# Moved tile copies, four prologue means and an earlier split of the fourth gate weight in a two-layer decoder trunk

## The chip, the cores and the metric

The kernel runs on one core of one Trainium2 chip. The metric is the device time of one execution in microseconds, as a median of repeated runs. TensorE is the matrix engine, ScalarE, VectorE and GpSimd work on tiles of 128 partitions, SyncE (SP) issues the DMA transfers. Each engine goes through its own instructions in order, and they wait for each other by counting semaphores.

## The reference

```
for i in (0, 1):                       # 512 tokens, width 1024
    h = rmsnorm(x, norm_pre[i])
    y = fox_mixer(h) if i == 0 else conv_mixer(h)      # attention with forget gates; gated short convolution
    x = x + rmsnorm(y, norm_post[i])                   # residual update
    gate = sigmoid(rmsnorm(x, pe_norm[i]) @ pe_w_gate[i])
    x = x + gate * (p[i] @ pe_w_proj[i])               # p[i]: 256 wide, per-layer embedding
```

`fox_mixer` projects `h` to q, k, v, z and 16 forget gates, `conv_mixer` to four tensors of width 1024; both end with an output projection of 1024 x 1024. All is in float32.

## The kernel before, in words

The residual stream is kept transposed in `xT`, as KT = 8 tiles of 128 features by 512 tokens. Each float32 operand of a matrix product is split into a rounded high part (`_hi`) and a rest (`_lo`), and a product is three matmuls of 128x512: hi·hi, lo·hi, hi·lo (lines 1031 to 1033). A weight tile of 1024x128 (a *slot*) is loaded into one of two `w_raw` buffers, ScalarE casts it to one of four `w_hi` buffers (`weight_hi`, line 470), and GpSimd subtracts to get `w_lo` (`weight_lo`, line 410); in the output projection VectorE does this subtraction (`slot_lo`, line 894). A load waits until the slot two before it has its low part, and a cast waits until TensorE has done with the slot four before it.

**Prologue.** For each of the eight tiles ScalarE makes `act_hi` (line 489) and for six of them a square `x_sq` (line 492); VectorE makes `act_lo` (line 730), and squares tiles 3 and 5 itself (line 735) and adds tiles 2 and 4 to them (line 738). TensorE runs two matmuls per tile for the forget gates (lines 1055, 1056) and six mean matmuls with `mean_f`, a matrix of 1/1024, that sum the squares over features (line 1066; each counts as two instructions in the trace). Then come the first two projection steps (lines 1073 to 1077). Ahead of all of it ScalarE casts the gates' weights `f_w` (line 484), and TensorE runs eleven matmuls on constants.

**Tail of a layer.** Each layer ends with the output projection (eight steps of 24 matmuls), the embedding's projection `ple_tile` (eight tiles of six matmuls; four stay in PSUM, the last four go through the two banks `ps_pj` and are copied to `pleT` by `ple_copy`, line 652), and the gate stage: gate tiles 0, 1 and 2 side by side, feature tile by feature tile of `act`, as `act` comes (`side_by_side`), then a mean (`norm_mean`), then tiles 3 to 7 one after the other. While TensorE is in the embedding's projection, the residual update runs: ScalarE turns the mean of the squares into a scale (lines 498, 500), VectorE computes `t_a` = `yT` times scale (line 926) and `xT` += `t_a` (line 917), ScalarE makes `act_hi` (line 657) and squares (lines 614, 618), VectorE makes `act_lo` (line 921), and GpSimd adds the squares up (`add_square`, line 445). TensorE needs `act_lo` k for the k-th part of the gate tiles, and the sum for the mean behind them.

The orders of ScalarE and VectorE are written out by hand. In the update of the kernel before, ScalarE copies embedding tile 0 ahead of the first `act_hi`, tile 1 behind `act_hi` 0, tiles 2 and 3 behind `act_hi` 1 (`PLE_COPY_AT`), and casts the fourth gate weight (slot `SLOT_GATE[l] + 3`) behind the fifth square; GpSimd makes its low part behind its fourth addition. In the last layer the last gate tile is done in two halves of 256 tokens (`parts`): `gate_scale` (line 952) for both, and then, half by half, tanh on ScalarE (line 700), two VectorE instructions (lines 967, 970) and a store.

Of the kernel before, what the change touches and what calls it, by code (L numbers as in the profile page):

```python
# [82 lines left out]
GROUPS = 16  # L83
PLE_COPY_AT = {0: [1], 1: [2, 3]}
P_AT = 4
NORM_AFTER = KT - 3
PAIRED = {2: 3, 4: 5}
MEANS = [k for k in range(KT) if k not in PAIRED]
TURN_0_WEIGHTS = {5: [0], 8: [1], 14: [2, 3]}
# [20 lines left out]
def tile_step(first, m):  # L110

    return first + m - (m > WIDE)


def trunk(nc, xT_in, pT_in, weights, f_in, b_f_in, pre_in, post_in, pe_in, taps_in, outT):
# [6 lines left out]
    with ctx:  # L122
# [3 lines left out]
        def sem(name):  # L126
            return ctx.enter_context(nc.semaphore(name))
# [107 lines left out]
        x_sq_act = sem("x_sq_act")  # L235
        x_sq_dve = sem("x_sq_dve")
        x_pair = sem("x_pair")
        act_hi_done = sem("act_hi_done")
# [150 lines left out]
        def _(pool):  # L389
# [12 lines left out]
            def weight_lo(slot, place):  # L402

                pool.wait_ge(w_hi_done, slot + stream(place) - place + 1)
                if place in [slot + 3 for slot in SLOT_GATE]:

                    pool.wait_ge(w_ready, stream(place))
                for k in range(0, KT, LO_TILES):
                    tiles = slice(k, k + LO_TILES)
                    last = nc.gpsimd.tensor_tensor(w_lo[place % RING][:, tiles], w_raw[stream(place) % RAW][:, tiles],  # L410
                                                   w_hi[place % RING][:, tiles], ALU.subtract)
                last.then_inc(w_ready, 1)
# [34 lines left out]
            for l in range(2):  # L447
                for m in range(KT):
                    add_square(3 * KT * l + KT + m)
                    if m == 4:  # L450
                        weight_lo(SLOT_GATE[l] + 3, SLOT_GATE[l] + 3)
                for m in range(KT):
                    for slot in ([4, 5] if m == 0 else [m + 5]):
                        if slot < KT + 3 * (l == 0):
                            weight_lo(SLOT_GATE[l] + slot, SLOT_GATE[l] + slot)
                if l == 0:
                    with pool.Fori(0, KT) as m:
                        for j in range(4):
                            weight_lo(4 * m + SLOT_CONV + 3 + j, SLOT_CONV + 3 + j)
# [3 lines left out]
        def _(act):  # L463
# [18 lines left out]
            log_exp_tables()  # L482
            act.wait_ge(f_loaded, 16)
            nc.scalar.copy(f_w[:, :, 0:F_PART], f_raw[:]).then_inc(f_hi_done, 1)
            act.wait_ge(g_loaded[0], 16)
            for k in range(KT):

                act.wait_ge(x_loaded[k], 16)
                nc.scalar.activation(act_hi[0][:, k, :], xT[:, k, :], ACT.Copy, scale=g_pre[:, 0, k:k + 1]
                                     ).then_inc(act_hi_done, 1)  # L490
                if k not in PAIRED.values():
                    nc.scalar.activation(x_sq[k][:], xT[:, k, :], ACT.Square).then_inc(x_sq_act, 1)
            weight_hi(0, 0)
# [126 lines left out]
            for l in range(2):  # L620
# [4 lines left out]
                for m in range(KT):  # L625
# [17 lines left out]
                    if m == P_AT:  # L643
                        act.wait_ge(p_loaded, 16 * l + 16)
                        nc.scalar.copy(p_hi[:], p_in[:]).then_inc(p_hi_done, 1)
                norm_scale(3 * l + 1, ps_o[:])
                act.wait_ge(g_loaded[3], 16)
# [5 lines left out]

                ple_copy(0)
                for m in range(KT):
                    act.wait_ge(x_new, 2 * KT * l + m + 1)
                    nc.scalar.activation(a_g[:, m, :], xT[:, m, :], ACT.Copy, scale=g_pe[:, l, m:m + 1]  # L657
                                         ).then_inc(act_hi_done, 1)
                    for tile in PLE_COPY_AT.get(m, []):
                        ple_copy(tile)  # L660
                    square(3 * KT * l + KT + m, xT[:, m, :])
                    if m == 4:
                        weight_hi(SLOT_GATE[l] + 3, SLOT_GATE[l] + 3)

# [60 lines left out]
        @block.vector  # L725
        def _(dve):
            for k in range(KT):

# [3 lines left out]
                                               ).then_inc(act_ready, 1)  # L732
                if k in PAIRED.values():
                    pair = list(PAIRED.values()).index(k)
                    nc.vector.tensor_tensor(x_sq[k][:], xT[:, k, :], xT[:, k, :], ALU.mult).then_inc(x_sq_dve, 1)
                    dve.wait_ge(x_sq_act, k - pair)
                    dve.wait_ge(x_sq_dve, pair + 1)
                    nc.vector.tensor_tensor(x_sq[k][:], x_sq[k - 1][:], x_sq[k][:], ALU.add).then_inc(x_pair, 1)

# [146 lines left out]
            for l in range(2):  # L886
# [15 lines left out]
                for m in range(KT):  # L902
# [6 lines left out]
                    if m == P_AT:  # L909
                        dve.wait_ge(p_hi_done, l + 1)  # L910
                        nc.vector.tensor_tensor(p_lo[:], p_in[:], p_hi[:], ALU.subtract).then_inc(p_ready, 1)
                dve.wait_ge(rs_ready, 3 * l + 2)
                links = {}
# [24 lines left out]

                def gate_scale(m):
                    if m < WIDE:  # L940
# [7 lines left out]
                    else:  # L948
                        for i, tokens in enumerate(parts(l, m)):
                            s = tile_step(STEP_GATE[l], m) + i  # L950
                            dve.wait_ge(pj_done, s + 1)
                            nc.vector.tensor_tensor(t_a[m % 2][:, tokens], ps_pj[s % 2][:, tokens], rs[:, tokens],
                                                    ALU.mult).then_inc(pj_free[s % 2], 1)

                gate_scale(0)
                for m in range(KT):
                    if m == 0:
                        gate_scale(1)
                    elif m > 1:
                        gate_scale(m)  # L960
# [3 lines left out]
                    gated = t_a[m % 2] if m < PLE_STEPS else ps_ple[m - PLE_STEPS]  # L964
                    for i, tokens in enumerate(parts(l, m)):
                        dve.wait_ge(g_tanh, KT * l + m + i + 1)
                        link = chain(nc.vector.scalar_tensor_tensor(gated[:, tokens], t_b[m % 2][:, tokens], 1.0,
# [56 lines left out]
        def _(pe):  # L1024
# [28 lines left out]
            for k in range(KT):  # L1053
# [4 lines left out]
                if k == KT - 1:  # L1058
                    end.then_inc(f_done, 1)
                summed = sum(paired < k for paired in PAIRED.values())  # L1060
                if k in PAIRED.values():
                    pe.wait_ge(x_pair, summed + 1)
                elif k not in PAIRED:
                    pe.wait_ge(x_sq_act, k - summed + 1)
                if k in MEANS:
                    end = nc.tensor.matmul(ps_o[:], mean_f[:], x_sq[k][:], start=k == MEANS[0], stop=k == KT - 1)
            end.then_inc(ms_done, 1)
# [219 lines left out]
```

## Time and profile before

| | us |
|---|---|
| median of 3 runs | 648.5 (648.17 to 648.59) |
| the profiled execution | 647.84 |
| its span in the trace | 646.0 |
| TensorE busy | 632.9 (98%) |
| VectorE busy | 388.1 (60%) |
| ScalarE busy | 322.5 (50%) |
| GpSimd busy | 308.2 (48%) |

The span runs from the first instruction to the last, the execution's own time has a further 1.8 us around it. A line such as L921 is the line of the kernel. A row of a timeline gives the start and the duration, the engine, the line and the operation, what is written from what, and in brackets the idle time of the engine before it and who ended it. The chain is followed back from the last instruction, at each step to what released it.

### The profile page before, as it was taken

How to read it: one execution, taken by the hardware profiler on the slowest of the kernel's cores; microseconds unless marked ns; L12 is line 12 of the kernel's file. 1: busy time of each engine (PE TensorE's matmuls, PEld its weight loads, DVE VectorE, ACT ScalarE, POOL GpSimd, SP SyncE). 2: the span in 40 equal slices, each digit the busy share in tenths (PEclk: the TensorE clock that was granted, in tenths of full speed). 3: DMA queues.
4: the chain of work that ended last, by engine and by line, in shares of the span. 5: the costliest groups of instructions: out<-in, count | busy, mean ns of one | idle time of the engine just before them, and what ended most of it. 6: DMA issues, size and time to landing. Idle time of an engine off the chain costs nothing.

```text
span 646.0 us, 9283 instructions
## 1 busy us (share of the span) xinstructions
PE 632.9 (98%) x2932; PEld 517.4 (80%) x2932; DVE 388.1 (60%) x774; ACT 322.5 (50%) x557; POOL 308.2 (48%) x412
## 2 busy tenths in 40 slices
PE   8999999999999999999989999999999999999897
PEld 5788888888888888788767788888888887887686
DVE  5558678787878787455868635333434242456864
ACT  6748566565657575555665632321222122555451
POOL 1776554645545566000566558556544651001770
PEclk9999999999999999999999999999999999999999
DMA  6363334343334333153013223323222422350131
GB/s 203 109 203 109 107 106 134 116 110 111 116 112 127 125 106 107 33 195 131 2 60 104 97 74 122 117 78 130 74 94 92 129 99 97 97 164 32 33 131 65
DMA packets 27161, 68.69 MB, mean 106 GB/s; under 512 B 3568, under 2 KB 10096, under 8 KB 27136
## 3 DMA queue, kind: packets, MB, share of 16 engines
q1 hardware_dynamic: 27136, 68.37, 32.3%
q8 instruction: 14, 0.23, 0.2%
q14 instruction: 11, 0.09, 0.0%
HBM read 66.23 MB, written 2.13 MB: 106 GB/s over the span
## 4 chain that ended last, share of the span: by engine, by line
PE 90%; DVE 7%; ACT 2%; issue 1%; DMA 0%; SPq 0%; DVEq 0%
PE ps_pj L1031 25%; PE ps_pj L1033 25%; PE ps_pj L1032 25%; PE ps_tr L1040 3%; DVE act_lo L921 2%; PE ps_o L1142 2%; PE ps_o L1141 2%; PE ps_sc L1111 1%; DVE xT L917 1%; PE ps_sc L1109 1%; PE ps_tr L1031 1%; PE ps_tr L1033 1%; PE ps_tr L1032 1%; DVE t_a L926 1%; PE ps_o L1046 1%
## 5 line engine op out<-in xcount | busy, mean ns | idle before, releaser
L410 POOL TENSOR_TENSOR w_lo<-w_raw,w_hi 128x256 fp32r<-128x256 f32 x324 | 253.5, 816 | 127.4 <-ACT w_hi L470 117.9
L1031 PE MATMUL ps_pj<-act_hi,w_hi 128*128 128x512 f32 (+1 forms) x728 | 290.2, 399 | 5.4 <-DVE act_lo L921 4.3
L1033 PE MATMUL ps_pj<-act_hi,w_lo 128*128 128x512 f32 (+1 forms) x728 | 282.8, 389 | 0.0
L1032 PE MATMUL ps_pj<-act_lo,w_hi 128*128 128x512 f32 (+1 forms) x728 | 282.7, 388 | 0.0
L1031 PEld LDWEIGHTS ps_pj<-act_hi,w_hi 128*128 128x128 f32 x728 | 137.0, 188 | 36.5 <-DVE act_lo L921 7.9
L1033 PEld LDWEIGHTS ps_pj<-act_hi,w_lo 128*128 128x128 f32 x728 | 136.8, 188 | 28.7
L1032 PEld LDWEIGHTS ps_pj<-act_lo,w_hi 128*128 128x128 f32 x728 | 137.2, 188 | 24.5 <-issue 0.7
L470 ACT CAST w_hi<-w_raw 128x1024 fp32r<-128x1024 f32 x96 | 100.5, 1048 | 92.5 <-DMA w_raw<-in_weights 69.7
L445 POOL TENSOR_TENSOR acc<-acc,sq 128x512 f32<-128x512 f32 x14 | 21.3, 1525 | 115.4 <-ACT sq L618 114.6
L418 POOL TENSOR_TENSOR bias<-bias,future 128x128 f32<-128x128 f32 x64 | 32.1, 533 | 76.0 <-DMA bias<-negc_scratch 76.0
L525 ACT ACTIVATE logit<-logit,nmax 128x128 f32<-128x128 f32 (+1 forms) x64 | 36.0, 563 | 46.4 <-DVE nmax L766 46.0
L781 DVE TENSOR_TENSOR pt_lo<-ps_tr,pt_hi 128x128 fp32r<-128x128 f32 (+1 forms) x64 | 30.8, 483 | 9.7 <-ACT pt_hi L535 8.9
L894 DVE TENSOR_TENSOR w_lo<-w_raw,w_hi 128x1024 fp32r<-128x1024 f32 x15 | 18.4, 1226 | 25.2 <-ACT w_hi L470 25.2
L766 DVE CUSTOM_DVE_ANT_0 logit<-ps_sc,bias 128x128 f32<-128x128 f32 (+1 forms) x64 | 31.2, 488 | 3.0 <-issue 1.5
L775 DVE TENSOR_SCALAR logit<-logit,rrec 128x128 f32<-128x128 f32 (+1 forms) x64 | 30.3, 473 | 2.3
L535 ACT CAST pt_hi<-ps_tr 128x128 fp32r<-128x128 f32 (+1 forms) x64 | 26.8, 423 | 4.7 <-PE ps_tr L1040 3.8
L1040 PE MATMUL ps_tr<-ident,logit 128*128 128x128 f32 x160 | 28.2, 275 | 0.1
L1008 DVE TENSOR_TENSOR cv_z<-ps_pj,rs 128x512 f32<-128x512 f32 x8 | 5.5, 692 | 38.0 <-PE ps_pj L1033 38.0
L827 DVE TENSOR_TENSOR q_lo<-scaled,q_hi 64x512 fp32r<-64x512 f32 x32 | 26.5, 828 | 1.9 <-ACT q_hi L565 1.5
L1040 PEld LDWEIGHTS ps_tr<-ident,logit 128*128 128x128 f32 x160 | 20.6, 140 | 7.7 <-DVE logit L775 1.4
L988 DVE TENSOR_TENSOR cv_w<-ps_pj,cv_c 128x512 f32<-128x512 f32 x8 | 5.5, 692 | 31.2 <-PE ps_pj L1033 31.1
L921 DVE SCALAR_TENSOR_TENSOR act_lo<-xT,g_pe,act_hi 128x512 fp32r<-128x512 f32 x16 | 20.9, 1317 | 5.2 <-ACT act_hi L657 5.2
(143 smaller groups left out, 741.4 us busy)
## 6 DMA issues: line engine op xcount, KB each, us to landing
w_raw<-in_weights SPq DMA_DIRECT2D x100, 512.0 KB, 3.4
bias<-negc_scratch SPq DMA_DIRECT2D x16, 256.0 KB, 7.4
bias<-negc_scratch SPq DMA_DIRECT2D x16, 192.0 KB, 6.2
xT<-in_xT SPq DMA_DIRECT2D x8, 256.0 KB, 4.4
bias<-negc_scratch SPq DMA_DIRECT2D x16, 128.0 KB, 4.8
out<-xT SPq DMA_DIRECT2D x7, 256.0 KB, 2.0
bias<-negc_scratch SPq DMA_DIRECT2D x16, 64.0 KB, 3.4
p_in<-in_pT SPq DMA_DIRECT2D x2, 512.0 KB, 4.6
```

The source lines that it names most:

```text
L410: last = nc.gpsimd.tensor_tensor(w_lo[place % RING][:, tiles], w_raw[stream(place) % RAW][:, tiles], w_hi[place % RING][:, tiles], ALU.sub ...
L418: nc.gpsimd.tensor_tensor(diagonal, diagonal, future[:], ALU.add).then_inc(bias_ready[h], 1)
L470: nc.scalar.copy(w_hi[place % RING][:], w_raw[position % RAW][:]).then_inc(w_hi_done, 1)
L525: nc.scalar.activation(logit[b][:, 0:n], logit[b][:, 0:n], ACT.Exp, scale=-1.0, bias=nmax[:, b:b + 1], accum_out=rsum[:, b:b + 1]).then_in ...
L766: nc.vector.tensor_tensor_reduce(out=logit[b][:, 0:n], in0=ps_sc[u % 2][:, 0:n], in1=bias[h][:, i, 0:n], scale=-1.0, scalar=3e38, op0=ALU. ...
L775: nc.vector.tensor_scalar(logit[b][:, 0:n], logit[b][:, 0:n], rrec[:, b:b + 1], None, ALU.mult).then_inc(prob_ready, 1)
L781: nc.vector.tensor_tensor(causal(pt_lo, i), ps_tr[n % TR_BANKS][:, 0:(i + 1) * P].rearrange("p (k c) -> p k c", c=P), causal(pt_hi, i), AL ...
L921: nc.vector.scalar_tensor_tensor(a_g[1][:, m - 1, :], xT[:, m - 1, :], g_pe[:, l, m - 1:m], a_g[0][:, m - 1, :], ALU.mult, ALU.subtract).t ...
L1031: nc.tensor.matmul(out, w_h, a[0][:, k, tokens], start=k == first, stop=False)
L1032: nc.tensor.matmul(out, w_h, a[1][:, k, tokens], start=False, stop=False)
L1033: end = nc.tensor.matmul(out, w_l, a[0][:, k, tokens], start=False, stop=k == last)
L1040: last = nc.tensor.transpose(ps_tr[n % TR_BANKS][:, t * P:(t + 1) * P], tile, ident[:])
```

## The change

- ScalarE's prologue: `act_hi` 0 goes first, the cast of `f_w` behind it; ScalarE squares all eight tiles.
- VectorE no longer squares; it adds up squares 0 and 1, then 2 and 1's sum into 3, then 4 into 5 (four additions). TensorE runs four means, for tiles 3, 5, 6 and 7.
- Residual update, in both layers: the copies of the embedding tiles 0, 1 and 3 stand behind `act_hi` 1, 2 and 3, the one of tile 2 behind square 2.
- The fourth gate weight is cast by ScalarE ahead of the norm's scale, and VectorE makes its low part ahead of the update, where GpSimd did so in the midst of it.
- The last gate tile of the last layer: each half is scaled right ahead of its own gating, instead of both halves first.

```diff
-PLE_COPY_AT = {0: [1], 1: [2, 3]}
+PLE_COPY_AT = {1: [0], 2: [1], 3: [3]}
+PLE_COPY_BEHIND = {2: [2]}
-PAIRED = {2: 3, 4: 5}
-MEANS = [k for k in range(KT) if k not in PAIRED]
+SUMS = {1: [0], 3: [2, 1], 5: [4]}
+MEANS = {3: 3, 5: 4}
...
             def weight_lo(slot, place):
 
                 pool.wait_ge(w_hi_done, slot + stream(place) - place + 1)
-                if place in [slot + 3 for slot in SLOT_GATE]:
+                if place in [slot + 4 for slot in SLOT_GATE]:
 
                     pool.wait_ge(w_ready, stream(place))
...
                     add_square(3 * KT * l + KT + m)
-                    if m == 4:
-                        weight_lo(SLOT_GATE[l] + 3, SLOT_GATE[l] + 3)
...
             log_exp_tables()
-            act.wait_ge(f_loaded, 16)
-            nc.scalar.copy(f_w[:, :, 0:F_PART], f_raw[:]).then_inc(f_hi_done, 1)
             act.wait_ge(g_loaded[0], 16)
             for k in range(KT):
 
                 act.wait_ge(x_loaded[k], 16)
                 nc.scalar.activation(act_hi[0][:, k, :], xT[:, k, :], ACT.Copy, scale=g_pre[:, 0, k:k + 1]
                                      ).then_inc(act_hi_done, 1)
-                if k not in PAIRED.values():
-                    nc.scalar.activation(x_sq[k][:], xT[:, k, :], ACT.Square).then_inc(x_sq_act, 1)
+                if k == 0:
+                    act.wait_ge(f_loaded, 16)
+                    nc.scalar.copy(f_w[:, :, 0:F_PART], f_raw[:]).then_inc(f_hi_done, 1)
+                nc.scalar.activation(x_sq[k][:], xT[:, k, :], ACT.Square).then_inc(x_sq_act, 1)
...
+                weight_hi(SLOT_GATE[l] + 3, SLOT_GATE[l] + 3)
                 norm_scale(3 * l + 1, ps_o[:])
...
-                ple_copy(0)
                 for m in range(KT):
...
                     square(3 * KT * l + KT + m, xT[:, m, :])
-                    if m == 4:
-                        weight_hi(SLOT_GATE[l] + 3, SLOT_GATE[l] + 3)
+                    for tile in PLE_COPY_BEHIND.get(m, []):
+                        ple_copy(tile)
...
-                if k in PAIRED.values():
-                    pair = list(PAIRED.values()).index(k)
-                    nc.vector.tensor_tensor(x_sq[k][:], xT[:, k, :], xT[:, k, :], ALU.mult).then_inc(x_sq_dve, 1)
-                    dve.wait_ge(x_sq_act, k - pair)
-                    dve.wait_ge(x_sq_dve, pair + 1)
-                    nc.vector.tensor_tensor(x_sq[k][:], x_sq[k - 1][:], x_sq[k][:], ALU.add).then_inc(x_pair, 1)
+                for other in SUMS.get(k, []):
+                    dve.wait_ge(x_sq_act, k + 1)
+                    wait(dve, x_sum, added)
+                    nc.vector.tensor_tensor(x_sq[k][:], x_sq[other][:], x_sq[k][:], ALU.add).then_inc(x_sum, 1)
+                    added += 1
...
+                slot_lo(SLOT_GATE[l] + 3)
                 dve.wait_ge(rs_ready, 3 * l + 2)
...
                 for m in range(KT):
+                    whole = len(parts(l, m)) == 1
                     if m == 0:
                         gate_scale(1)
-                    elif m > 1:
+                    elif m > 1 and whole:
                         gate_scale(m)
...
                     for i, tokens in enumerate(parts(l, m)):
+                        if not whole:
+                            gate_scale(m, i)
                         dve.wait_ge(g_tanh, KT * l + m + i + 1)
...
                 if k in MEANS:
-                    end = nc.tensor.matmul(ps_o[:], mean_f[:], x_sq[k][:], start=k == MEANS[0], stop=k == KT - 1)
+                    pe.wait_ge(x_sum, MEANS[k])
+                elif k >= 6:
+                    pe.wait_ge(x_sq_act, k + 1)
+                if k in MEANS or k >= 6:
+                    end = nc.tensor.matmul(ps_o[:], mean_f[:], x_sq[k][:], start=k == 3, stop=k == KT - 1)
```

## Rows read from the trace of the kernel before

**Rows 1.** The chain that ended last: its share of the span by engine.
```profile
PE 90%; DVE 7%; ACT 2%; issue 1%; DMA 0%; SPq 0%; DVEq 0%
```

**Rows 2.** The chain in order of time, prologue: start, us, what.
```profile
1.19 0.42 SPq L334
...
1.66 2.93 DMA f_raw<-in_f_weights
...
5.64 0.52 ACT x_sq L492
6.16 0.61 ACT act_hi L489
...
11.23 1.32 DVE act_lo L730 x2
...
14.01 1.13 PE ps_o L1066 x2
...
16.91 0.86 PE ps_o L1066 x2
...
21.41 1.81 PE ps_pj L1077 x8
```

**Rows 3.** The same chain, around the gate stages: start, us, what.
```profile
312.71 0.59 ACT pleT L652
...
328.44 0.50 PE ps_pj L1031
...
332.81 0.86 PE ps_o L1046 x2
...
613.40 0.86 PE ps_o L1046 x2
```

**Rows 4.** Timeline of all engines, the last half tile.
```profile
641.87 0.42 DVE L952 TENSOR_TENSOR t_a<-ps_pj,rs 128x256 f32<-128x256 f32 x1 [2.45 <-PE ps_pj L1033]
...
642.33 0.42 ACT L700 ACTIVATE t_b<-t_a 128x256 f32<-128x256 f32 x1 [2.46 <-DVE t_a L952]
...
643.46 0.42 DVE L970 SCALAR_TENSOR_TENSOR xT<-ps_tr,xT 128x256 f32<-128x256 f32 x1
```

**Rows 5.** Timeline of ScalarE, layer 0, norm and start of the update.
```profile
303.83 0.60 ACT L498 ACTIVATE ln_ms<-ps_o 128x512 f32<-128x512 f32 x1 [1.73 <-PE ps_o L1046]
...
308.69 0.59 ACT L652 COPY pleT<-ps_pj 128x512 f32<-128x512 f32 x1 [3.62 <-PE ps_pj L1033]
309.17 0.73 ACT L657 ACTIVATE act_hi<-xT,g_pe 128x512 fp32r<-128x512 f32 x1
```

**Rows 6.** Timeline of VectorE, layer 0, residual update.
```profile
305.10 0.69 DVE L926 TENSOR_TENSOR t_a<-yT,ps_o 128x512 f32<-128x512 f32 x1 [2.85 <-ACT ps_o L500]
...
316.39 1.07 DVE L917 TENSOR_TENSOR xT<-xT,t_a 128x512 f32<-128x512 f32 x1
317.39 1.78 DVE L921 SCALAR_TENSOR_TENSOR act_lo<-xT,g_pe,act_hi 128x512 fp32r<-128x512 f32 x1
```

**Rows 7.** Timeline of GpSimd, layer 0, residual update.
```profile
313.90 4.71 POOL L445 TENSOR_TENSOR acc<-acc,sq 128x512 f32<-128x512 f32 x3 [55.06 <-ACT sq L618]
...
320.27 4.17 POOL L410 TENSOR_TENSOR w_lo<-w_raw,w_hi 128x256 fp32r<-128x256 f32 x4
```

**Rows 8.** Groups of instructions by line (x count, busy us, mean ns).
```profile
L470 ACT CAST w_hi<-w_raw 128x1024 fp32r<-128x1024 f32 x96 | 100.5, 1048 | 92.5 <-DMA w_raw<-in_weights 69.7
...
L894 DVE TENSOR_TENSOR w_lo<-w_raw,w_hi 128x1024 fp32r<-128x1024 f32 x15 | 18.4, 1226 | 25.2 <-ACT w_hi L470 25.2
```

**Rows 9.** Timeline of the DMA queue of SP, layer 0.
```profile
297.16 0.33 SPq L321 DMA_DIRECT2D w_raw<-in_weights  x1
```

**Rows 10.** The loads of line 321, 280 to 400 us: issue to landing.
```profile
DMA to landing us min/median/max: 3.2/3.3/5.6
```

**Rows 11.** DMA issue of the norm gains: x count, KB, us to landing.
```profile
g_pre<-in_norm_pre SPq DMA_DIRECT2D x1, 8.0 KB, 2.5
```

**Rows 12.** Stages: us, busy us of PE, PEld, DVE, ACT, POOL; clock, DMA.
```profile
13.00:14.00 1.00, 0.33 (x2) 0.00 (x0) 0.90 (x3) 0.99 (x2) 0.00 (x0) 1.00 0.00 0
```

More of the change, by code:

```diff
@@ L235, in trunk @@
         x_sq_act = sem("x_sq_act")
-        x_sq_dve = sem("x_sq_dve")
-        x_pair = sem("x_pair")
+        x_sum = sem("x_sum")
         act_hi_done = sem("act_hi_done")
@@ L726, in _ @@
         def _(dve):
+            added = 0
             for k in range(KT):
@@ L937, in gate_rest, with gate_scale @@
                         add_square(2 * KT + m)
-                def gate_scale(m):
+                def gate_scale(m, i=0):
                     if m < WIDE:
@@ L948, in gate_scale @@
                     else:
[L949 to L953, printed above, removed]
+                        s = tile_step(STEP_GATE[l], m) + i
+                        tokens = parts(l, m)[i]
+                        dve.wait_ge(pj_done, s + 1)
+                        nc.vector.tensor_tensor(t_a[m % 2][:, tokens], ps_pj[s % 2][:, tokens], rs[:, tokens],
+                                                ALU.mult).then_inc(pj_free[s % 2], 1)
                 gate_scale(0)
                 for m in range(KT):
+                    whole = len(parts(l, m)) == 1
                     if m == 0:
                         gate_scale(1)
-                    elif m > 1:
+                    elif m > 1 and whole:
                         gate_scale(m)
@@ L1059, in _ @@
                     end.then_inc(f_done, 1)
[L1060 to L1064, printed above, removed]
-                if k in MEANS:
-                    end = nc.tensor.matmul(ps_o[:], mean_f[:], x_sq[k][:], start=k == MEANS[0], stop=k == KT - 1)
+                if k in MEANS:
+                    pe.wait_ge(x_sum, MEANS[k])
[3 more added lines that the diff above has]
+                    end = nc.tensor.matmul(ps_o[:], mean_f[:], x_sq[k][:], start=k == 3, stop=k == KT - 1)
             end.then_inc(ms_done, 1)
```

## Prediction

> **What bounds the kernel now.** I read the chain that ended last first. It lies on TensorE for nine tenths [rows 1], so a change pays only where the chain leaves TensorE. Read in order of time, it does that in three kinds of place that this change touches. In the prologue it runs through ScalarE and VectorE to the sixth `act_lo`, and reaches the first projection's matmul at 17.77 [rows 2]. Between a layer's output projection and its gate stage it runs through VectorE's residual update, until the seventh `act_lo` releases TensorE at 328.44; the mean behind the gate's first three tiles starts at 332.81 in layer 0 and at 613.40 in layer 1 [rows 3]. At the end it is the last half tile's gating [rows 4]. The timelines of ScalarE, VectorE and GpSimd in the second place then show why VectorE is late there [rows 5 to 7].
>
> **Residual update, twice: what goes.** Today ScalarE takes `ple_copy(0)` ahead of the first `act_hi`. That copy waits 3.62 us for TensorE, runs at 308.69, and `act_hi` follows at 309.17 [rows 5], though the first new `xT` was there at about 306.5 (the first `t_a` starts at 305.10 and takes 0.69 with the update as long behind it [rows 6]). After the change ScalarE can write `act_hi` 0 at 306.5 to 307.1, some 2.7 us earlier. The second thing that goes is the fourth gate weight's low part on GpSimd, 4.17 us in the middle of the update [rows 7].
>
> What GpSimd costs VectorE must be worked out, because GpSimd's seven additions per layer stay. An `xT` update takes 0.69 us alone and 1.07 beside GpSimd; an `act_lo` took 1.78 there [rows 6], where its chain piece in the prologue, without GpSimd, is 1.32/2 = 0.66 [rows 2]. `t_a`, whose second input is in PSUM, is not stretched. Three additions in a row take 4.71 us [rows 7] with two VectorE instructions of about 0.6 let in between, so one holds the path for (4.71 - 1.2)/3 = 1.17, call it 1.2 us. The two engines take turns, whole instructions at a time. The Trainium skill says the same and more strongly (SBUF — State Buffer, "SBUF: two separate sides"): the pair of ports is an exclusive lock, held for the whole instruction, also against a VectorE instruction with two SBUF inputs. By that rule every addition that meets such an instruction delays it until it ends; by a mere stretching in proportion, an addition would cost some 0.5 us and the update would end about 2 us earlier than below. The walk below takes turns as the rows do.
>
> **The walk through layer 0.** VectorE per tile is `xT` 0.61, `act_lo` 0.66, `t_a` 0.61 and gaps, 2.0 us. From 305.10 [rows 6]: `xT` 0 and 1 done at 306.45 and 307.75, `act_lo` 0 at 308.4, 1 at 310.35. The first square is at ScalarE's end at 309.7, behind the moved copy 0; its addition gets its turn at 310.35 to 311.55. Taking turns from there (additions 2 to 6 at 312.15, 314.0, 317.75, 319.6 and 322.7, each 1.2; an `xT` or `act_lo` that is ready meanwhile waits, a square is ready about 1.3 behind its `xT`), `act_lo` 2 ends at 314.0, 3 at 316.5, 4 at 319.6, 5 at 322.1, 6 at 325.2 and 7 at 325.85, and the last addition at 327.0. TensorE: 8 x 9 = 72 matmuls for three tiles side by side, at 1.81/8 = 0.226 us [rows 2]. The first three run at once, the fourth needs the bank of copy 3, which starts at 312.71 and takes 0.59 [rows 3]. That copy now stands behind `act_hi` 3, whose `xT` comes at 312.15, so it still runs at about 312.75; the fourth matmul ends at some 313.9, a restart included, and without a stall the other 68 end at 329.3. Tile 6 is then wanted at 329.3 - 18 x 0.226 = 325.2, just as it comes; with 0.2 for a restart the mean starts at 329.5 in place of 332.81, **3.3 us earlier**. Bounds: no stall gives 3.5. If each of the six additions ahead of `act_lo` 6 cost its whole 1.2 us (308.4 + 6 x 2.0 + 7.2 = 327.6 in place of 328.44), 0.85 us is left. I take 3.3, since an addition that falls on `t_a` costs about half. The mean needs all additions (327.0), so it is not the next wait. Layer 1 has the same walk: 6.6 us for both.
>
> **What is added ahead of the update.** ScalarE gets one weight cast of 1.05 us and VectorE one low part of 1.23 [rows 8]. Before `ln_ms` at 303.83 ScalarE waits 1.73 us [rows 5], so the cast fits at 302.1 to 303.1 if its load has landed. The load is issued at 297.16 [rows 9] and loads take 3.2 to 5.6 us there, 3.3 in the median [rows 10], thus 300.5. VectorE does its part at 303.2 to 304.4, and sits idle for the 2.85 us before 305.10 [rows 6]. Cost nothing, with 0.7 us to spare on both; queued behind is the whole update, so past 302.8 a late load would cost one for one. Of the moved copies, 1 frees its bank at about 310.85, and TensorE starts the tile that needs it six matmuls before 312.71, at 311.3; 2 frees its own at 311.9 for the gate's first tile, which starts at about 312.5. Both are in time. SP issues no more than before: the load two slots on starts earlier, since the fourth weight's parts are ready 20 us sooner, and nothing waits for it.
>
> **Prologue.** ScalarE no longer waits for `f_raw` (4.59, from 1.66 + 2.93 [rows 2]) before `act_hi` 0. The norm gains land at 1.19 + 2.5 = 3.7 [rows 2, 11], tile 0 issued before them too. So `act_hi` 0 runs 3.75 to 4.4, the cast of `f_w` 4.6 to 4.9, square 0 to 5.45. Tile 1's `act_hi` stands at 6.16 in the chain now, straight behind a square; its load sets some start between 5.45 and that, I take 5.85. From there one tile is 0.61 + 0.52 = 1.13 us [rows 2], eight squares instead of six (+1.04 us of ScalarE): `act_hi` 7 ends at 13.25, square 7 at 13.8, the first weight at 14.8. VectorE loses two squares and two sums and gets four sums, 4 instructions for 4, each of 0.69 (the form of [rows 6]). Its order gives the third sum at 10.85, `act_lo` 4 and 5 at 11.5 and 12.2, sum 4 at 12.85, `act_lo` 6 and 7 at 13.5 and 14.15. TensorE has four means of 0.86 instead of six, 1.7 us less: mean 3 starts at 10.9 and takes 1.13 as one behind a wait does, two tiles of gates at 0.46 each, then mean 5 at 12.95, gate 6, mean 6, gate 7, mean 7 until 16.45, in place of 16.91 + 0.86 = 17.77 [rows 2]. **1.3 us earlier.** Bounds: 0.5 if every handover costs a further 0.1, 1.6 if all that is gone is the two means. `ms_done`, the forget gates' chain, GpSimd's low parts and the loads behind them are released by this and move with it; the first low part has 3.6 us of matmuls before its use, so it does not become the wait.
>
> **Tail.** Today the first half's two instructions stand between the last `t_a` half (641.87) and the second half's [rows 4]. After: 641.87 + 0.42, tanh to 642.75, two instructions of 0.42 with gaps, 643.66 in place of 643.88. 0.2 us (0 to 0.5).
>
> **Sum.** 1.3 + 6.6 + 0.2 = 8.1 us. The profiled execution took 647.84 with a span of 646.0; it becomes 639.7. The median of the runs is 0.66 above it, so I predict **640.4 us**.
>
> **Rivals.**
> 1. The additions pace the update: they now begin four microseconds sooner and may meet VectorE on every tile. Against it, only `xT` and `act_lo` are stretched in the rows. Gain 0.85 per layer, in all 1.3 + 1.7 + 0.2 = 3.2: 645.3. Chance 0.13.
> 2. TensorE's clock falls in the prologue. Its work between 7 and 11 us thins to eight short matmuls, with a wait of about 1 us ahead of mean 3. Against it: it was busy for 0.33 of a microsecond at 13 to 14 and the granted clock stayed 1.00, the 2.4 GHz level [rows 12]. At the 1.2 GHz level the 5.55 us of work from 10.9 on would cost 2.8 to 5.6 more: 643.2 to 646.0. The Trainium skill (TensorE: Matmul & The Clock Gate, "Why this matters for your kernels") warns that idle gaps between bursts send the clock back; the row so far speaks for a safe gap. Chance 0.08.
> 3. Part is given back later: a gate step or a weight load in layer 0 doesn't follow, a load of 5.6 us in place of 3.3 [rows 10] takes 2.3 us: 642.7. For each later wait I find a releaser that moves too, which speaks against it. Chance 0.10.
> 4. Slower: the fourth weight's load lands late and its cast holds `ln_ms`, at its new place ahead of the norm. It costs nothing until 302.8 and then one for one in both layers. To lose 8.1 us and 1.3 more it would have to land (8.1 + 1.3)/2 = 4.7 us after that, 10.3 us from its issue; the longest is 5.6 [rows 10]. Chance 0.04, about 650.5.
> 5. No change: VectorE's update isn't what the gate stage waits for, 648.5. The release at 328.44 speaks against it. Chance 0.03.
>
> **Numbers.** My forecast holds 0.62, by itself 638.9 to 642.2. The range of 638.8 to 644.5 takes in rivals 2 (its nearer half) and 3 and leaves out 1, 4 and 5. Within 0.2%, 1.3 us, is about what a measurement can't tell from no change. Faster: 0.62 + 0.13 + 0.08 + 0.10 = 0.93; same 0.03; slower 0.04.
>
> **What would show it.** Right: first projection matmul at about 16.5; `act_hi` 0 of the update some 2.7 us earlier against `ln_ms`; no wait for `act_lo` on TensorE above 0.4 us in the gate stages; from `ln_ms` (303.83) to the mean (332.81) 25.6 us in place of 29.0; the last half tile's store alone at the end. Wrong: `act_lo` still of 1.2 to 1.8 us with TensorE waiting behind it (rival 1), matmuls of twice the length about 11 us (2), `ln_ms` later than 1 us behind its mean (4), or a gate stage shortened and a longer wait behind it (3).

## The result and the profile after

The changed kernel took 641.75 us in the median of four runs (639.91 to 642.9), the kernel before 648.34 beside it: a ratio of 0.9895, with a 95% interval of 0.9872 to 0.9919. Forecast were 640.4 us and a range of 638.8 to 644.5. The median is thus 6.6 us lower, where 8.1 were forecast. The four runs had a mean granted clock of 0.997 (641.69 us), 0.997 (642.9), 1.0 (641.8) and 0.998 (639.91). The profiled execution took 641.69 us with a span of 639.9, 6.1 us shorter than before.

The chain that ended last, by engine and by line, says first where VectorE's share of 7% went:

```profile
PE 91%; POOL 3%; issue 2%; DVE 1%; ACT 1%; DMA 1%; SPq 0%; POOLq 0%; DVEq 0%
```

VectorE has left the chain but for 1%; GpSimd's 3% are new, and lie between 20 and 44 us. Now the same chain in order of time around the gate stages and at the end, as in [rows 3, 4]:

```profile
303.69 0.86 PE ps_o L1048 x2
...
330.23 0.86 PE ps_o L1048 x2
...
580.90 0.86 PE ps_o L1048 x2
...
607.46 0.86 PE ps_o L1048 x2
635.94 0.43 DVE t_a L951
636.40 0.43 ACT t_b L698
636.85 0.44 DVE ps_tr L969
637.32 0.42 DVE xT L972
```

From the update's mean to the gate's mean it is 26.54 and 26.56 us, where it was 332.81 - 302.94 = 29.87 and 613.40 - 583.51 = 29.89: 3.33 us less in each layer, 6.66 for both. In the last half tile (`ps_tr` and `xT` are its two VectorE instructions) the last update ends at 637.74, 1.80 behind its `t_a`; in [rows 4] it was 643.88 - 641.87 = 2.01, so 0.21 less. Between the first gate mean and the update's mean of layer 1 nothing has moved, 250.67 us against 250.70. That leaves the start, and there the kernel is later than before: the update's mean of layer 0 comes 0.75 us after 302.94. Here is the prologue in the stages' view (us, then busy us of PE, PEld, DVE, ACT, POOL, the granted clock and DMA) and in TensorE's timeline:

```profile
6.00:7.00 1.00, 0.68 (x2) 0.19 (x2) 0.40 (x1) 1.00 (x3) 0.00 (x0) 1.00 0.96 336
7.00:8.00 1.00, 0.59 (x2) 0.19 (x2) 1.00 (x3) 1.00 (x3) 0.00 (x0) 1.00 1.04 385
8.00:9.00 1.00, 0.42 (x3) 0.19 (x2) 0.75 (x2) 1.00 (x3) 0.00 (x0) 1.00 1.07 406
9.00:10.00 1.00, 0.68 (x4) 0.19 (x2) 1.00 (x2) 1.00 (x3) 0.00 (x0) 1.00 1.04 416
10.00:11.00 1.00, 0.35 (x2) 0.00 (x0) 0.90 (x3) 1.00 (x2) 0.00 (x0) 1.00 1.05 430
11.00:15.00 4.00, 3.93 (x7) 1.86 (x8) 3.27 (x6) 3.82 (x7) 0.04 (x1) 0.57 0.12 50
15.00:17.77 2.77, 2.77 (x11) 1.41 (x9) 0.00 (x0) 0.34 (x1) 2.76 (x4) 1.00 0.00 0
```

```profile
11.07 1.80 PE L1067 MATMUL ps_o<-x_sq,mean_f 128*128 128x512 f32 x2 [0.72 <-DVE x_sq L735]
11.88 1.42 PE L1057 MATMUL ps_sc<-act_hi,f_w 128*64 128x512 f32 x1
13.09 0.63 PE L1058 MATMUL ps_sc<-act_lo,f_w 128*64 128x512 f32 x1
13.52 0.63 PE L1057 MATMUL ps_sc<-act_hi,f_w 128*64 128x512 f32 x1
...
17.69 0.79 PE L1074 MATMUL ps_pj<-act_hi,w_hi 128*128 128x512 f32 x1
```

From 6 to 11 us TensorE is busy for a third to two thirds of each microsecond, and then the granted clock falls to its lower level: 0.57 in the mean of 11 to 15 us, 1.00 again from there. The mean behind the wait takes 1.80 us where [rows 2] has 1.13, a matmul of 512 columns 0.63 in the timeline (0.43 in the chain) where it had 0.39 (0.23). The durations of neighbours overlap in a timeline, and the chain counts each share once. The mean ahead of the first projection matmul ends at 17.77 in the chain of before, and at 18.26 here.

### The profile page after: what moved, and what is told of

Its sections match the earlier page's. It is cut to its first block, busy times and chain, and to the rows that moved or that the text cites. A ratio compares the mean times of both kernels' runs of the same rounds, so it can differ in the third digit from the quotient of the medians.

```text
span 639.9 us, 9274 instructions
## 1 busy us (share of the span) xinstructions
PE 629.9 (98%) x2928; PEld 516.4 (81%) x2928; DVE 385.4 (60%) x776; ACT 324.1 (51%) x559; POOL 298.8 (47%) x404
## 4 chain that ended last, share of the span: by engine, by line
PE 91%; POOL 3%; issue 2%; DVE 1%; ACT 1%; DMA 1%; SPq 0%; POOLq 0%; DVEq 0%
PE ps_pj L1033 25%; PE ps_pj L1035 25%; PE ps_pj L1034 25%; PE ps_tr L1042 3%; POOL w_lo L410 2%; PE ps_o L1143 2%; PE ps_o L1142 2%; PE ps_sc L1112 1%; PE ps_tr L1033 1%; PE ps_tr L1035 1%; PE ps_tr L1034 1%; PE ps_sc L1110 1%; PE ps_o L1067 1%; PE ps_o L1048 1%; DMA xT<-in_xT 1%
## 5 line engine op out<-in xcount | busy, mean ns | idle before, releaser
L410 POOL TENSOR_TENSOR w_lo<-w_raw,w_hi 128x256 fp32r<-128x256 f32 x316 | 241.1, 796 | 132.7 <-ACT w_hi L468 132.7
L418 POOL TENSOR_TENSOR bias<-bias,future 128x128 f32<-128x128 f32 x64 | 33.9, 561 | 73.2 <-DMA bias<-negc_scratch 73.2
L892 DVE TENSOR_TENSOR w_lo<-w_raw,w_hi 128x1024 fp32r<-128x1024 f32 x17 | 20.8, 1226 | 26.2 <-ACT w_hi L468 26.2
L825 DVE TENSOR_TENSOR q_lo<-scaled,q_hi 64x512 fp32r<-64x512 f32 x32 | 24.1, 754 | 1.9 <-ACT q_hi L563 1.5
L785 DVE TENSOR_TENSOR o_u<-ps_o,o_half 64x512 f32<-64x512 f32 x16 | 11.0, 688 | 22.7 <-ACT o_half L542 22.5
```

The source lines that it names most:

```text
L418: nc.gpsimd.tensor_tensor(diagonal, diagonal, future[:], ALU.add).then_inc(bias_ready[h], 1)
```

## The experiments

The first four kernels below (`filled` to `prologue_only`) ran on one chip and the other eight on another. The kernel before took 648.01 us on the first, 647.93 and 647.86 on the second, and 648.34 beside the result; each median stands beside before's on the same chip.

**Where the clock comes in: four changes of the prologue.** `filled` gives TensorE something to do while it waits:

```diff
                 if k == KT - 1:
                     end.then_inc(f_done, 1)
+                for _ in range({0: 3, 1: 2, 2: 1, 3: 3}.get(k, 0)):
+                    nc.tensor.matmul(ps_tr[1][:, 0:P], mean_f[:], mean_f[:], start=True, stop=True)
```

> The changed kernel with nine more matmuls of 128x128 in the prologue, behind the forget gates' matmuls of tiles 0 to 3, three, two, one and three of them; their results are used nowhere. Theory (the clock fell because TensorE had too little to do between 6 and 11 us): the granted clock stays at 1.00 over 11 to 15 us, the first mean takes 0.86 to 1.13 instead of 1.80, the first projection matmul starts at about 16.5 instead of 18.26, and the median is 1.6 to 1.9 us below the changed kernel's, about 640.0, with less spread from run to run. Rival (the clock falls for another cause, or the delay is ScalarE's): no change, or 0.2 to 1 us slower for the extra work: 641.8 to 642.8.

Measured: 640.74 us (639.2 to 641.82, four runs), before 648.01; ratio 0.9882 (0.9867 to 0.9896). The mean granted clock was 0.999 or 1.0 in each run, and the first projection matmul was at 16.70 in the timeline, where the changed kernel had 17.69. So the clock held in these four runs, and in the prologue of the profiled one the microsecond came back. In time this does not show: 7.3 us below before is between the changed kernel's 6.6 and the 8.1 of its second measurement (`after_again` below), and the intervals overlap. The spread did not shrink, though that was expected too. The profiled execution, at 641.82 the slowest, shows another loss, behind the prologue (who TensorE waited for, 17 to 68 us; and its timeline there):

```profile
PE ps_tr L1042 <- DVE logit L773: 1.2, 1, 1.2
```

```profile
51.29 0.66 PE L1042 MATMUL ps_tr<-ident,logit 128*128 128x128 f32 x4 [1.18 <-DVE logit L773]
```

`logit` is a tile of attention weights, which VectorE normalises (line 773) ahead of TensorE's transposes. The same view of the kernel before shows no wait for it. It is taken up below.

`six_means` keeps TensorE busy with work that is wanted anyway, and spares VectorE two sums:

```diff
-SUMS = {1: [0], 3: [2, 1], 5: [4]}
-MEANS = {3: 3, 5: 4}
+SUMS = {3: [2], 5: [4]}
+MEANS = {3: 1, 5: 2}
...
-                elif k >= 6:
+                elif k not in (2, 4):
                     pe.wait_ge(x_sq_act, k + 1)
-                if k in MEANS or k >= 6:
-                    end = nc.tensor.matmul(ps_o[:], mean_f[:], x_sq[k][:], start=k == 3, stop=k == KT - 1)
+                if k not in (2, 4):
+                    end = nc.tensor.matmul(ps_o[:], mean_f[:], x_sq[k][:], start=k == 0, stop=k == KT - 1)
```

> The changed kernel with six means again (tiles 0, 1, 3, 5, 6, 7) and two sums on VectorE, all eight squares on ScalarE. Clock theory: the two means lie at 7 to 9 us and keep TensorE busy, so the clock stays at 1.00; mean 3 waits for one sum instead of three and starts at about 10.2, and the first projection matmul comes at 16.2 to 16.6: median 639.7 to 640.3. Rival (what costs is ScalarE's longer order): as the changed kernel, 641.7.

Measured: 639.89 us (638.68 to 640.48), before 648.01; ratio 0.9872 (0.9857 to 0.9886), no clock below 0.999. The median lies 8.1 us below before with two means more of work; against the changed kernel's 0.9895 (0.9872 to 0.9919) the intervals overlap, and the two are set side by side further down.

`old_prologue` is the changed kernel with the prologue of before, `prologue_only` the reverse; both diffs are those of the change, taken apart.

> The changed kernel with the prologue of the kernel before. Clock theory: the clock does not fall, the first projection matmul is at 17.77 as before, both gate stages gain 3.3 and the tail 0.2: 648.34 - 6.8 = 641.5, that is 0.2 us below the changed kernel and less spread. Rival (the prologue gained its 1.3 us and something later lost it): 643.0.

Measured: 641.14 us (640.93 to 641.43), before 648.01; ratio 0.9897 (0.9883 to 0.9911). The rest of the change gives 6.87 us, and all runs lie within 0.5 us.

> The kernel before with only the prologue of the change. Clock theory: the first projection matmul at 18.2 instead of 17.77 and a further 0.4 by the transfers that move with it: 648.5 to 649.3, with a spread of some 2 us between runs as the changed kernel has. Rival (the prologue gained 1.3 us): 647.0.

Measured: 647.58 us in the median of twelve runs, before 648.01; ratio 1.0003 (0.9991 to 1.0015), no difference (in the mean 648.02, before 647.89). But they fall in two groups: eight with a mean clock of 0.999 or 1.0 at 646.48 to 648.56, 647.2 in the mean, and four with 0.994 to 0.997 at 649.01 to 650.36, 649.6 in the mean. The theory's two halves are both there, a gain of 0.7 us against before's mean, and 2.4 us more in the runs that lost the clock, and I had mistaken how they mix: I expected every run late. The profiled one kept its clock; its first projection matmul is at 16.45 in the timeline, against 17.21 before.

**Which edit shortens the gate stages.** `copies_only` is the kernel before with `PLE_COPY_AT`, `PLE_COPY_BEHIND` and their loops changed as in the change; `weight_only` with the casts and low parts of the fourth gate weight moved alone.

> The kernel before with only the embedding copies moved. Theory (turns on one path between VectorE and GpSimd): act_hi 0 comes 2.7 us sooner, the fourth weight's 4.17 us on GpSimd still stand in the middle and delay tiles 5 and 6; act_lo 6 comes some 2 to 2.7 us earlier: 4.0 to 5.4 us for both layers, 642.6 to 644.0 where before stands at 648.0. Rival (the copies alone suffice, TensorE is the bound at once): 3.3 a layer, 641.4.

Measured: 644.45 us (644.03 to 644.72), before 647.93; ratio 0.9946 (0.9933 to 0.996): 3.5 us, less than theory (4.0 to 5.4) and rival (6.6) had. From the update's mean to the gate's, the chain has 331.43 - 303.26 = 28.17 us, 1.7 less than before.

> The kernel before with only the fourth gate weight's cast and low part moved. Theory: the start of the update stays, GpSimd loses 4.17 us of its 15.3 in it; the tile period falls from 2.9 to 2.7 for two tiles and the pile of additions goes: 0.4 to 1.0 us a layer, 646.0 to 647.2. Rival (GpSimd's low part was the main cost): 2.5 to 3.3 a layer, 641.4 to 643.0. A rival on the other side: the cast ahead of the norm's scale holds it, 648.5 or more.

Measured: 645.16 us (644.12 to 645.59), before 647.93; ratio 0.9958 (0.9945 to 0.9972): 2.8 us, twice the middle of the 0.8 to 2.0 that I gave it, and less than the rival's 5.0 to 6.6; from mean to mean it is in layer 0 331.60 - 302.95 = 28.65, 1.2 less, in layer 1 28.39, 1.5 less. VectorE's timeline shows by what. First `copies_only`, then `weight_only`, both in layer 0:

```profile
316.12 0.74 DVE L923 SCALAR_TENSOR_TENSOR act_lo<-xT,g_pe,act_hi 128x512 fp32r<-128x512 f32 x1
...
318.11 1.79 DVE L923 SCALAR_TENSOR_TENSOR act_lo<-xT,g_pe,act_hi 128x512 fp32r<-128x512 f32 x1
...
320.52 1.22 DVE L919 TENSOR_TENSOR xT<-xT,t_a 128x512 f32<-128x512 f32 x1
321.66 1.23 DVE L923 SCALAR_TENSOR_TENSOR act_lo<-xT,g_pe,act_hi 128x512 fp32r<-128x512 f32 x1
...
323.52 1.77 DVE L919 TENSOR_TENSOR xT<-xT,t_a 128x512 f32<-128x512 f32 x1
325.21 3.46 DVE L923 SCALAR_TENSOR_TENSOR act_lo<-xT,g_pe,act_hi 128x512 fp32r<-128x512 f32 x2
```

```profile
317.62 1.78 DVE L919 SCALAR_TENSOR_TENSOR act_lo<-xT,g_pe,act_hi 128x512 fp32r<-128x512 f32 x1
...
321.03 0.74 DVE L919 SCALAR_TENSOR_TENSOR act_lo<-xT,g_pe,act_hi 128x512 fp32r<-128x512 f32 x1
...
323.01 1.78 DVE L919 SCALAR_TENSOR_TENSOR act_lo<-xT,g_pe,act_hi 128x512 fp32r<-128x512 f32 x1
...
326.41 1.62 DVE L919 SCALAR_TENSOR_TENSOR act_lo<-xT,g_pe,act_hi 128x512 fp32r<-128x512 f32 x2
```

With the low part still on GpSimd (its four pieces run from 319.29 to 323.49, two additions back to back right behind them until 326.42), each `act_lo` and each `xT` update from 320.5 us on is held: 1.22 and 1.23 beside the pieces, 1.77 and 3.46 for two beside the additions. Only `t_a` keeps its 0.67. Without it `act_lo` 3 and 5 are held (1.78), while 4 takes 0.74 and the last two 1.62 together. The two edits add up to 6.3 us of the 6.9; neither makes TensorE the bound by itself.

> The kernel before with only the last gate tile's halves reordered. Theory: 0.2 us, 647.8 where before stands at 648.0, not to be told from no change by time; in the trace 0.22 us less between the last matmul and the last update. Rival (nothing, since the store ends last): 0.0.

Its edit is that of `gate_scale` and its calls. Measured: 647.67 us in the median of eleven runs (647.16 to 648.15), before 647.93; ratio 0.9997 (0.9988 to 1.0006). By time it is no difference; in its own chain the last update ends 643.72 - 641.93 = 1.79 us behind the start of the last `t_a`, 0.22 less than the 2.01 of [rows 4].

**Is it the thin work that makes the clock fall?** `two_means_out` takes two means away from the kernel before and touches nothing else:

```diff
-                if k in MEANS:
-                    end = nc.tensor.matmul(ps_o[:], mean_f[:], x_sq[k][:], start=k == MEANS[0], stop=k == KT - 1)
+                if k in MEANS[2:]:
+                    end = nc.tensor.matmul(ps_o[:], mean_f[:], x_sq[k][:], start=k == MEANS[2], stop=k == KT - 1)
```

> The kernel before without its first two mean matmuls, those of tiles 0 and 1: this leaves two eighths of the features out of the first norm's mean; the orders of ScalarE and VectorE stay. Theory (TensorE's thin work up to the first sum lets the clock fall): in a third of the runs the mean granted clock is 0.997 or less and those runs take 2 to 2.5 us more than the others, which stay at 648.0. Rival (the clock falls by ScalarE's new order, or by the wait for three sums): no run below 0.998, all at 648.0.

Measured: 648.44 us in the median of eleven runs (647.86 to 649.04), before 647.93; ratio 1.0007 (0.9998 to 1.0016). Two runs of eleven had a mean clock of 0.997, none of the kernel before's 21 on that chip was below 0.999. That points to the means, with ScalarE's and VectorE's order untouched; but two of 11 against none of 21 could also be chance, and where in those two executions the clock was low isn't known. Those two took 648.62 and 648.23, no more than the others: my 2 to 2.5 us were wrong here. In this kernel TensorE waits for VectorE twice behind 11 us (before does so too, and [rows 12] is one of those stretches), and slower matmuls could lie in the waits; that isn't shown.

The profiled execution of `two_means_out` kept its clock, and it is the one that speaks most against a simple reading. Its first mean stands at 11.72, and ahead of it TensorE had a little less to do than in the changed kernel's first profile (2.62 us of work from 6 to 11 against 2.72, and 0.28 in the microsecond behind) and waited longer (up to 0.92 us, for `act_lo`):

```profile
6.00:7.00 1.00, 0.42 (x2) 0.19 (x2) 0.43 (x1) 0.66 (x2) 0.00 (x0) 1.00 1.01 295
7.00:8.00 1.00, 0.23 (x1) 0.00 (x0) 0.75 (x1) 1.00 (x3) 0.00 (x0) 1.00 0.93 361
8.00:9.00 1.00, 0.64 (x2) 0.19 (x2) 0.62 (x1) 1.00 (x3) 0.00 (x0) 1.00 1.03 322
9.00:10.00 1.00, 0.65 (x2) 0.19 (x2) 0.62 (x2) 1.00 (x2) 0.00 (x0) 1.00 0.96 365
10.00:11.00 1.00, 0.68 (x2) 0.19 (x2) 0.89 (x3) 1.00 (x3) 0.00 (x0) 1.00 1.03 418
11.00:12.00 1.00, 0.28 (x1) 0.28 (x2) 1.00 (x2) 1.00 (x3) 0.00 (x0) 1.00 1.01 414
```

The granted clock is 1.00 in each of these rows and to 15 us. So thin work does not by itself bring the fall in an execution.

The last four ran side by side. `after_again` is the changed kernel, `six_again` the one with six means.

> The changed kernel unaltered, on the same chip and beside the same runs as the three below. Clock theory: runs with a mean granted clock of 0.997 or less occur, one in three or more, and lie 1.5 to 2.5 us above the fastest; median 1 to 2 us above six_again. Rival (the difference to the version with six means was between chips): within 0.4 us of it, no fallen clock.

Measured: 639.78 us (638.79 to 641.04), before 647.86; ratio 0.9882 (0.9864 to 0.9899). One run of four had a clock of 0.997 and is the slowest by 1.25 us. The profiled execution is one that kept its clock, and thus shows the prologue as I had walked through it, in the chain:

```profile
10.50 1.12 PE ps_o L1067 x2
...
12.55 1.00 PE ps_o L1067 x2
...
14.02 0.86 PE ps_o L1067 x2
...
15.34 0.86 PE ps_o L1067 x2
16.20 0.23 PE ps_pj L1074
```

The first projection matmul is at 16.20, its span 637.0 us. Tile 1 of `xT` landed at 2.12 + 3.13 = 5.25 here and at 5.82 in the first profile; with that load the same course would end at 16.77, 1.0 us before 17.77, and by this estimate the first profile's 18.26 has 1.5 us of clock in it.

> The version with six means a second time, beside the changed kernel. Clock theory: no run below 0.998, median 8.0 us under the kernel before, 639.9 where that stands at 648.0. Rival: as the changed kernel.

Measured: 638.87 us (638.49 to 639.24), before 647.86; ratio 0.9859 (0.9841 to 0.9877). 0.9 us under the changed kernel, with half the spread and no clock below 0.999.

`five_means` adds one sum to that:

```diff
-SUMS = {3: [2], 5: [4]}
-MEANS = {3: 1, 5: 2}
+SUMS = {3: [2], 5: [4], 7: [6]}
+MEANS = {3: 1, 5: 2, 7: 3}
...
-                elif k not in (2, 4):
+                elif k not in (2, 4, 6):
```

The condition of the matmul below it changes alike.

> The version with six means, and square 6 added to 7 on VectorE so that five means are left (tiles 0, 1, 3, 5, 7). At the prologue's end TensorE runs its means one after the other; one less there gives up to 0.4 us (mean 7 starts behind a sum at about 15.4 and not at 16.1), 639.5. Rival (the sum is the new last wait): the same as with six, 639.9, or 0.3 more.

Measured: 639.28 us (638.59 to 639.71); ratio 0.987 (0.9852 to 0.9887). The interval covers six_again's, so the fifth sum isn't shown to give or cost anything.

`two_squares_out` is the version with six means without those of tiles 0 and 1 (`not in (0, 1, 2, 4)` in both conditions, `start=k == 3`).

> The changed kernel with four means (tiles 3, 5, 6, 7) and only two sums, 2 into 3 and 4 into 5; the squares of tiles 0 and 1 are left out of the first norm's mean. TensorE's thin work between 6 and 10 us stays, the wait for the third sum goes. Clock theory: the clock still falls in some runs (mean clock 0.997 or less), and those take 1.5 to 2.5 us more; the others are at 639.0 to 639.6. Rival (the wait for three sums alone makes it fall): no run below 0.998.

Measured: 639.41 us (638.6 to 640.69); ratio 0.9865 (0.9848 to 0.9883), no run of four below 0.999. By my own expectation that speaks for the rival, but four runs can miss an event that comes once in four. The two slower runs, 640.69 and 640.09, had a clock of 1.0, so runs differ by 2 us without a mean clock below 0.999 too.

Counted over all runs of which the clock is listed:

| kernels | runs | mean clock 0.997 or less |
|---|---|---|
| four means and nothing else for TensorE (the changed kernel twice, prologue_only, two_means_out, two_squares_out) | 35 | 9 |
| all others | 85 | 0 |

The 85 are 44 runs of the kernel before, 41 of `old_prologue`, `copies_only`, `weight_only`, `tail_only`, `filled`, `six_means`, `six_again` and `five_means`. The bound of 0.997 was chosen after seeing the runs; the 85 go down to 0.998.

## Why the prediction was right, and where it was off

**Both gate stages: right, 3.3 us a layer as forecast.** The two edits, tried alone and together, leave no other cause for it. The steps stand in the changed kernel's timelines of ScalarE, VectorE and GpSimd, layer 0, which answer to [rows 5 to 7]:

```profile
302.74 1.05 ACT L468 CAST w_hi<-w_raw 128x1024 fp32r<-128x1024 f32 x1
304.58 0.60 ACT L496 ACTIVATE ln_ms<-ps_o 128x512 f32<-128x512 f32 x1 [0.80 <-PE ps_o L1048]
...
307.36 0.72 ACT L655 ACTIVATE act_hi<-xT,g_pe 128x512 fp32r<-128x512 f32 x1 [1.54 <-DVE xT L916]
```

```profile
303.82 1.23 DVE L892 TENSOR_TENSOR w_lo<-w_raw,w_hi 128x1024 fp32r<-128x1024 f32 x1 [0.82 <-ACT w_hi L468]
305.85 0.69 DVE L925 TENSOR_TENSOR t_a<-yT,ps_o 128x512 f32<-128x512 f32 x1 [0.80 <-ACT ps_o L498]
...
316.55 0.74 DVE L920 SCALAR_TENSOR_TENSOR act_lo<-xT,g_pe,act_hi 128x512 fp32r<-128x512 f32 x1
...
318.53 1.79 DVE L920 SCALAR_TENSOR_TENSOR act_lo<-xT,g_pe,act_hi 128x512 fp32r<-128x512 f32 x1
...
323.93 3.48 DVE L920 SCALAR_TENSOR_TENSOR act_lo<-xT,g_pe,act_hi 128x512 fp32r<-128x512 f32 x2
```

```profile
310.58 3.53 POOL L445 TENSOR_TENSOR acc<-acc,sq 128x512 f32<-128x512 f32 x2 [51.39 <-ACT sq L616]
314.79 1.29 POOL L445 TENSOR_TENSOR acc<-acc,sq 128x512 f32<-128x512 f32 x1 [0.68 <-ACT sq L616]
```

All stand 0.75 us later than in the walk, by the start. The cast lies in ScalarE's wait and leaves 0.80 of it; VectorE's low part does the same with 0.80 left, where I had given 0.7 to both. `act_hi` 0 comes 307.36 - 304.58 = 2.78 us behind `ln_ms`, where it was 309.17 - 303.83 = 5.34: 2.56 sooner, forecast 2.7. `act_lo` 3 ends at 317.2 (the walk, 0.75 later: 317.25), 4 at 320.2 (320.35) and 7 at 327.4 (326.6), 0.8 late, and yet before TensorE wants it at 330.23 - 9 x 0.226 = 328.2. VectorE is stretched as much as ever, 1.79 in the worst case; what changed is that it happens sooner than TensorE needs the tile. TensorE's only wait of the stage for another engine is for copy 3, 0.2 us, and "no wait for `act_lo` above 0.4" held. The times fit turns by whole instructions, as [rows 6, 7] had it: where an addition lies in the way, `act_lo` takes 1.0 us more (1.79 against 0.74), and where none does, nothing; the 0.5 us an addition of a stretching in proportion is not what came. Of rival 1 (0.85 a layer) nothing came.

What I had wrong was how the two edits share this, which the prediction left open and the expectations put at 2.0 to 2.7 us a layer for the copies and 0.4 to 1.0 for the weight: alone they give 1.7 and 1.4. I had named the pile of additions behind the 4.17 us on GpSimd and priced it too low: it holds each `act_lo` and `xT` update in turn.

**Tail: right**, 0.21 us for 0.2.

**Prologue: the term of the sum that was mis-sized.** I had it at 1.3 us earlier and it was 0.49 later in the profiled execution, 1.8 us off, with 0.40 more lost by 67 us and 0.14 of that back by the update's mean (0.75 later). Over runs the term came to nothing in the mean of `prologue_only` (648.02, before 647.89), and to 0.7 in its eight runs with full clock. Three parts:

1. *The clock, my rival 2 with a chance of 0.08.* It took 1.5 us of that execution by the estimate above, and a mean clock of 0.997 or less came in 9 of 35 runs of kernels with four means and in none of 85 others. I had argued from [rows 12] that 0.33 of busy time in one microsecond left the clock alone. That row was one thin microsecond beside full ones; the change makes five thin ones in a row, and I read the rival's own sentence ("thins to eight short matmuls") without letting it move the chance. The wait ahead of the mean was 0.72 us where before had 0.70, so it does not tell the two apart. The Trainium skill (TensorE: Matmul & The Clock Gate, "Why this matters for your kernels") warns there of long idle gaps between bursts. Here no gap was longer than 0.72 us and the clock fell; the measured fall decides.
2. *Handovers.* With its clock kept, and the load of tile 1 as in the first profile, the gain is 1.0 and not 1.3 (mean 3, behind the third sum, at 11.07 instead of 10.9, mean 5 as much later, and another 0.15 between it and the end).
3. *A wait further on, in the way of rival 3.* Between the first projection and 67 us the profiled execution lost another 0.40 us, and the wait of `PE ps_tr` for `DVE logit` is 0.4; `filled` had 1.2, `two_squares_out` 0.6, `prologue_only` 0.2. In this execution GpSimd's first four bias additions start at 39.13, where they did at 37.76, and ScalarE's cast ahead of that `logit`, which waits for its weight load, at 47.99 instead of 47.22; in `filled` the cast is at 48.40, and the weight loads from 17 to 50 us took 4.7 us in the median (3.8 before). In the other three the store of the forget gates' sums, which the bias loads stand behind, took 4.4 to 4.5 us, where it took 3.3 before. Such a store isn't enough: it took 4.6 us in `two_means_out`, which has no such wait. Nor is it TensorE's earlier start, since in this execution TensorE was later than before. Why the transfers take longer in some executions is open. The same stretch also gives: in `after_again` the update's mean comes at 300.74, 2.2 us before 302.94, and only 1.6 of that (17.77 - 16.20) is from the prologue.

The whole comes out within the range since the two gains that carried the sum were right, 6.8 of 8.1 us forecast and 6.87 measured in `old_prologue`, and since the range reached to 644.5. In `after_again`, with three of four clocks kept, the median gain was 647.86 - 639.78 = 8.1 us, the forecast's own figure; by the walk with full clock it is 1.0 and not 1.3 from the prologue, so the exact match has luck in it.

**What stays open.** That thin work favours the fall rests on a count (9 of 35 against 0 of 85) in which two of the nine are from `two_means_out`, which changes only TensorE's work. Against it stand its profiled execution, thinner than the changed kernel's and at full clock, and `two_squares_out` with none in four. Where the clock fell is seen in one execution; of the other eight only the mean is known. What else has to be there for a fall wasn't found. Nor does the clock explain all of the first measurement: one of its runs took 641.8 us with a mean clock of 1.0.

## What to carry to other kernels

Before taking work off TensorE in a stretch where it waits for others anyway, look at how busy it is there in every microsecond, and at the granted clock of many runs and not of one profile: keeping the two spared means, 1.7 us of matmuls, cost no time that could be measured, and without them a mean clock of 0.997 or less came in a quarter of the runs. Six means gave 638.87 us against 639.78 side by side; the two intervals (0.9841 to 0.9877 and 0.9864 to 0.9899) still overlap, but none of its eight runs lost the clock, so it is the version I would keep. Where GpSimd and VectorE both work from SBUF, count the GpSimd instructions in VectorE's stretch and where the next engine needs each tile; one moved out of it also keeps the others from piling up behind it (1.2 to 1.5 us a layer here, with 4.17 us moved). And start the sequence that feeds the bound first: 2.6 us of a copy's wait ahead of `act_hi` cost 1.7 us a layer, measured by `copies_only`.

## What the runs showed of the hardware that was not expected

The granted clock fell from the 2.4 to the 1.2 GHz level without any wait of TensorE above 0.72 us, behind five microseconds in which it was busy for 0.68, 0.59, 0.42, 0.68 and 0.35, and it was back at the full level by 15.0, TensorE having been busy for 3.93 of the four microseconds before. It did so in some executions of a program and not in others: `after_again`, with 0.85, 0.52, 0.68, 0.68 and 0.50 in the same microseconds, kept it, and so did `two_means_out`, with 0.42, 0.23, 0.64, 0.65 and 0.68 there and waits of up to 0.92 us.
